# Alternating the two column halves of a tile's sums in the last matrix product of a decoder step

## The chip, the cores and the metric

The kernel runs on one core of a Trainium2 chip. The metric is the device time of one execution in microseconds (us); several executions are run and the median is quoted. One further execution was recorded by the hardware profiler, and all rows below are from it.

## The reference, cut to what matters

One decoder layer on 1024 prompt tokens and 32 sample tokens, `D_MODEL` 1024. It has a mixer part (gated linear attention beside a state-space model) and then PEER, a layer of 16384 single-neuron experts, of which each token uses 128. The change is in the second product of PEER:

```python
def block(args):
    xk, ik, gk = args
    act = jax.nn.gelu(jnp.einsum('tkd,td->tk', expert_u[ik], xk))
    return jnp.einsum('tk,tkd->td', gk * act, expert_v[ik])
...
x = x + peer_ffn(rmsnorm(x, norm2), peer_wq, peer_keys, peer_u, peer_v)
```

After it comes only the final RMSNorm of each token.

## The kernel before, in words

The first 2285 us hold the mixers, the expert scores, their top 16, and the first PEER product. They are not touched. The last part is `peer_down` (from L2347), about 1090 us.

**The product.** For six of the nine token tiles (ND = 6, 128 tokens each, the "dense" tiles) the kernel doesn't gather experts. It multiplies a weight matrix `w` (experts x tokens, mostly zeros) with the table `peer_v` (experts x 1024). The 16384 experts are 128 blocks of 128. Four blocks (GE = 4, counted by e) make a group, so there are 32 groups (NG, counted by g). In a group each dense tile s has 1024 sums for each of its tokens, which are two halves of 512 columns (W4), as a PSUM bank holds 512. So a group has 12 outputs (OUTS), numbered o = 2s + half. For each output and block there are three products (PARTS): every float32 operand is split into a high part h and a low part l in the fp32r type, and h*h, h*l and l*h are summed. That makes 4 x 3 = 12 products of 128x512 for each output, 144 in a group, 4608 in all. The stationary operand (the weight that PE loads) is the slice of `lo_wx` for the tile, the moving operand is half a row of `lo_vx`. The profile gives each product its own LDWEIGHTS record (engine PEld). Buffers come in two sets: even groups use lo_wx0 to 3 with up_ut2, up_ut0, up_ut1 and lo_vx3; odd groups use lo_wx4 to 7 with lo_vx4 to 7.

**PE's order** is written out in `peer_down`. Output after output, it waits until the bank is free (semaphore `o_added`; there are NPO = 6 banks `pd_po`), issues the 12 products and raises `o_done` with the last one. Ahead of each group it waits until VectorE (DVE) has made the low parts of all four blocks of that group: `v_lo` and `w_lo` must reach 4(g+1). Group 0 is a little different: its first six outputs run block by block.

**DVE's order** is also written out: for each group g and each output o (a "slot") one instruction that prepares group g+1, then the sum, then perhaps a gathered row:

```python
for g in range(NG):
    for o in range(OUTS):
        m = GE * (g + 1) + o // 3
        if g == 0:
            add(g, o)
        if m < NK:
            (lower.multiply, lower.low_v, lower.low_w)[o % 3](dve, m)
        if g >= 1:
            add(g, o)
        at = OUTS * g + o - FIRST_ROW
        for i in range(rows_by(at), rows_by(at + 1)):
            rows_v.add(dve, i, gate, acc_s)
```

`multiply` (L2132) forms `w` times the activations, `low_v` (L2147) the low part of a block of `peer_v`, `low_w` (L2152) the low part of `w`. `add` (L2471) waits for `o_done` of its output and adds the bank to `acc` in SBUF. `rows_v.add` (L1818) adds one gathered row of 1024 columns for the sparse tiles; 288 rows are spread evenly over 354 slots, from slot 0 of group 1 on. The last preparation for group g+1 is `low_w` in slot 11 of group g, right ahead of `add(g, 11)` and behind `add(g, 10)`.

**The others.** ScalarE (ACT) makes the high parts (L2137, L2141), SyncE (SP) loads `peer_v`, `w` and the activations, GpSimd (POOL) gathers the rows. In the last group nothing is left to prepare; PE first folds the sample tile with a small product (L2550), and DVE and ACT do the final norm of finished tiles between the sums, and of the last tile behind the last sum.

Of the kernel before, what the change touches and what calls it, by code (L numbers as in the profile page):

```python
# [11 lines left out]
F32R = mybir.dt.float32r  # L12
I32 = mybir.dt.int32
U32 = mybir.dt.uint32

P = 128
D = 1024
# [17 lines left out]
W4 = 512  # L35
# [1327 lines left out]
PARTS = ((0, 0), (0, 1), (1, 0))  # L1363
# [6 lines left out]
ND = 6  # L1370
# [467 lines left out]
def peer_topk(nc, s_sb, sel_t, u_d, up, lead, xs, idx, gate, raw):  # L1838


    with ExitStack() as ctx:
        def sb(name, shape, dt=F32):
            return ctx.enter_context(nc.sbuf_tensor("tk_" + name, shape, dt))
# [6 lines left out]
        top = sb("top", [P, PH, 2, TOPK])  # L1850
        ids = sb("ids", [P, PH, 2, TOPK], U32)
        idxf = sb("idxf", [P, PH, 2, TOPK])
        fin = sb("fin", [P, PH, TOPK])
        pos = sb("pos", [P, PH, TOPK], U32)
        pos2 = sb("pos2", [P, 2, PH, TOPK], U32)
        posf = sb("posf", [P, 2, PH, TOPK])
# [3 lines left out]
        sums = sb("sums", [P, PH])  # L1860
        idx_s = sb("idx_s", [P, NSEL], U32)
        gate_s = sb("gate_s", [P, NSEL])
# [219 lines left out]
GE = 4  # L2082
# [239 lines left out]
OUTS = 2 * ND  # L2322
# [16 lines left out]
def peer_down(nc, v_d, up, lead, lower, x2_tiles, acc, acc_s, idx, gate, raw, final_norm, y_tiles):  # L2339


    with ExitStack() as ctx:
# [3 lines left out]
        def sem(name):  # L2346
            return new_sem(nc, "pd_" + name)  # L2347

        lower.place(ctx, nc)
        vx, wx, mul, v_lo, w_lo = lower.vx, lower.wx, lower.mul, lower.v_lo, lower.w_lo  # L2350
        rows_v = Rows(ctx, nc, "dr", v_d, idx, 0, COLS, [lead.room[:, b] for b in range(3)], 2)
        NPO = 6
        po = [ctx.enter_context(nc.psum_tensor(f"pd_po{b}", [P, W4], F32)) for b in range(NPO)]
# [10 lines left out]
        o_done, o_added = sem("o_done"), sem("o_added")  # L2364
# [8 lines left out]
        @block.sync  # L2373
        def _(sp):
            def load(m):
                if m % 2 == 0 and m >= 4:
                    sp.wait_ge(w_lo, m - 2)
                    lower.load_wa(sp, m // 2)
                sp.wait_ge(v_lo, m - 1)
                lower.load_v(sp, m)  # L2380

            def load_acc(s):
                sp.dma_start(acc[:, s, :], x2_tiles[s]).then_inc(acc_in[s], 16)  # L2383

            load(2)
            load_acc(0)
            load(3)
            load_acc(1)
            up.keep(sp, NK - 1, 1)
            load_acc(2)  # L2390
            load(4)
            load_acc(3)
            load(5)
            load_acc(4)
            load_acc(5)
            up.all_kept(sp)
            load(6)
            load(7)
            for s in range(NSP):
                sp.dma_start(acc_s[:, s, :], x2_tiles[ND + s]).then_inc(accs_in, 16)  # L2400
            sp.wait_ge(accs_zero, 1)
            sp.dma_start(acc_s[0:TS, NSP, :], x2_tiles[NT - 1]).then_inc(accs_in, 16)
            for m in range(2 * GE, NK):
                load(m)
            sp.wait_ge(rows_v.used, COLS)
            sp.dma_start(gain, final_norm.rearrange("(o d) -> o d", o=1).broadcast_to([P, D])).then_inc(gain_loaded, 16)
            for i, s in enumerate(FINAL):
                sp.wait_ge(ready, i + 1)
                sp.dma_start(y_tiles[s], tile(s)).then_inc(written, 16)
            sp.wait_ge(written, 16 * NT)  # L2410
# [113 lines left out]

        @block.tensor
        def _(pe):
            def product(g, o, e):
                s, half = o // 2, o % 2
                for x, y in PARTS:
                    mm = nc.tensor.matmul(po[(OUTS * g + o) % NPO][:], wx[g % 2][e][y][:, s * P:(s + 1) * P],  # L2530
                                          vx[g % 2][e][x][:, half * W4:(half + 1) * W4],
                                          start=(e == 0 and (x, y) == PARTS[0]), stop=(e == GE - 1 and (x, y) == PARTS[-1]))
                return mm


            for e in range(GE):
                pe.wait_ge(v_lo, e + 1)
                pe.wait_ge(w_lo, e + 1)
                for o in range(NPO):
                    mm = product(0, o, e)  # L2540
                    if e == GE - 1:
                        mm.then_inc(o_done, 1)
            for g in range(NG):
                pe.wait_ge(v_lo, GE * (g + 1))
                pe.wait_ge(w_lo, GE * (g + 1))
                if g == NG - 1:
                    pe.wait_ge(shaped, PACK)
                    pe.wait_ge(rows_v.used, COLS)
                    for half in range(2):
                        nc.tensor.matmul(pf[half][0:TS, :], fold[:], acc_s[:, NSP, half * W4:(half + 1) * W4],  # L2550
                                         start=True, stop=True).then_inc(folded, 1)
                for o in range(NPO if g == 0 else 0, OUTS):
                    at = OUTS * g + o
                    if at >= NPO:
                        pe.wait_ge(o_added, at - NPO + 1)
                    for e in range(GE):
                        mm = product(g, o, e)
                    mm.then_inc(o_done, 1)


def mixers(nc, A, O, x_tiles, x2_tiles, ss2, lead):
# [24 lines left out]
def build(nc, A, O):  # L2586
# [10 lines left out]
    with nc.allow_non_contiguous_dma(reason="biases and S5 parameters, a few kilobytes"):  # L2597
        x2_order, y_order = [x2_tiles[t] for t in ORDER], [y_tiles[t] for t in ORDER]
        with ExitStack() as ctx:
# [4 lines left out]
            LIVE_SEMS.extend(lead.sems())  # L2604
            idx = ctx.enter_context(nc.sbuf_tensor("idx", [P, COLS], U32))
            gate = ctx.enter_context(nc.sbuf_tensor("gate", [P, COLS], F32))
# [48 lines left out]
```

## Time and profile before

| | us |
|---|---|
| three runs | 3372.06, 3375.76, 3374.07 |
| median | 3374.07 |
| profiled execution, its time | 3376.34 |
| its span | 3374.6 |
| PE busy in the span | 3285.9 (97%) |
| PEld busy | 2880.1 (85%) |
| DVE busy | 2551.5 (76%) |
| ACT, POOL busy | 901.1, 801.1 |
| granted TensorE clock, mean | 0.989 |

The busy time of PE counts each product from its start to its modelled end. Neighbouring products overlap, so a busy PE may still leave room, and the pace is read from the distance between two starts. The time outside the span is 1.74 us.

### The profile page before, as it was taken

The page shows a single profiled execution, that of the slowest core. Times are in us where ns is not written, and L with a number is a line of the kernel's source. Part 1 is how long each engine was busy: PE and PEld are TensorE (multiplying, and loading weights), DVE is VectorE, ACT ScalarE, POOL GpSimd, SP SyncE. Part 2 cuts the span into 40 slices and gives each one's busy share as a digit, 9 for nine tenths or more (in the row PEclk, how much of TensorE's full clock was granted, in tenths as well). Part 3 has the DMA queues.
Part 4 walks back from the last instruction along what each step waited for, and adds up shares of the span by engine and source line. Part 5 has one row for each costly group of instructions (what it writes and reads, how often), then busy time and mean ns, then how long its engine had stood idle before and what let it go on. Part 6 is the DMA issues. An engine that isn't in the chain of part 4 may idle for free. (4 is left out here: it accounts for less than half of the span.)

```text
span 3374.6 us, 46048 instructions
## 1 busy us (share of the span) xinstructions
PE 3285.9 (97%) x17796; PEld 2880.1 (85%) x17796; DVE 2551.5 (76%) x5349; ACT 901.1 (27%) x1310; POOL 801.1 (24%) x625
## 2 busy tenths in 40 slices
PE   8999989899999999999999999999999999999998
PEld 7867755499999999999999999997878888878787
DVE  6611253422499999989899888967999999999996
ACT  4210300211122222224444444432222222222222
POOL 0000000000001010113333333332444444444440
PEclk9999989899999999999999999999999999999999
DMA  3020021321144444448888888889899998988983
GB/s 98 14 39 27 13 91 59 119 57 38 55 136 136 147 144 145 137 150 303 289 316 309 287 326 285 329 310 339 309 307 312 311 311 310 311 315 309 312 307 132
DMA packets 332962, 695.58 MB, mean 206 GB/s; under 512 B 34332, under 2 KB 194936, under 8 KB 326584
## 3 DMA queue, kind: packets, MB, share of 16 engines
q1 hardware_dynamic: 248600, 386.28, 33.8%
q0 software_dynamic: 84144, 306.35, 26.4%
q8 instruction: 141, 2.31, 0.3%
q14 instruction: 77, 0.63, 0.1%
HBM read 580.10 MB, written 110.64 MB: 205 GB/s over the span
## 5 line engine op out<-in xcount | busy, mean ns | idle before, releaser
L1775 ACT ACTIVATE up_a<-up_pa 128x384 f32<-128x384 f32 x256 | 126.0, 492 | 838.9 <-PE up_pa L1760 829.2
L1799 POOL DMA_INDIRECT lead<-in_peer_v_dram,idx x174 | 259.7, 1492 | 361.8 <-DVE acc_s L1818 333.9
L2471 DVE TENSOR_TENSOR acc<-pd_po,acc 128x512 f32<-128x512 f32 x384 | 264.0, 688 | 101.6 <-PE pd_po L2530 97.4
L1799 POOL DMA_INDIRECT gr_row<-in_peer_u_dram,idx x192 | 229.0, 1193 | 374.4 <-DVE raw L1808 347.4
L1808 DVE CUSTOM_DVE_ANT_0 gr_row<-gr_row,xs 128x1024 f32<-128x1024 f32 x192 | 231.2, 1218 | 2.2 <-DMA gr_row<-in_peer_u_dram,idx 2.2
L1799 POOL DMA_INDIRECT dr_row<-in_peer_v_dram,idx x114 | 171.1, 1501 | 218.7 <-DVE acc_s L1818 215.3
L1818 DVE SCALAR_TENSOR_TENSOR acc_s<-lead,gate,acc_s 128x1024 f32<-128x1024 f32 x174 | 222.0, 1276 | 0.0
L2257 DVE TENSOR_SCALAR pg_hot_i<-pg_iota,sel_t 128x128 f32<-128x128 f32 x768 | 213.2, 353 | 0.0
L2292 PE MATMUL pg_pw<-pg_hot_i,pg_hot_j 128*128 128x128 f32 x1536 | 199.7, 275 | 1.5 <-DVE pg_hot_i L2257 1.5
L502 PE MATMUL fr_a<-pj_w,h_t 128*128 128x256 f32 (+1 forms) x864 | 200.0, 394 | 0.9 <-PEq L177 0.9
L502 PEld LDWEIGHTS fr_a<-pj_w,h_t 128*128 128x128 f32 (+1 forms) x864 | 170.9, 227 | 29.6 <-issue 8.2
L2292 PEld LDWEIGHTS pg_pw<-pg_hot_i,pg_hot_j 128*128 128x128 f32 x1536 | 192.5, 191 | 1.8 <-DVE pg_hot_i L2257 1.8
L2252 DVE TENSOR_TENSOR pg_hot_j<-pg_iota,sel_t 128x512 f32<-128x512 f32 x192 | 132.2, 688 | 79.2 <-PE pg_pw L2292 73.6
L1799 POOL DMA_INDIRECT lead<-in_peer_u_dram,idx x72 | 92.9, 1291 | 378.5 <-DVE raw L1808 302.8
L1750 PE MATMUL up_pt<-up_ident,lead 128*128 128x128 f32 x1024 | 134.9, 273 | 18.2 <-DVE up_ut1l L1780 4.5
L1818 DVE SCALAR_TENSOR_TENSOR acc_s<-dr_row,gate,acc_s 128x1024 f32<-128x1024 f32 x114 | 145.5, 1276 | 0.0
L1760 PE MATMUL up_pa<-h_dh,up_ut1h 128*128 128x384 f32 x688 | 140.8, 346 | 2.1 <-PEq L62 2.1
L1760 PE MATMUL up_pa<-h_dh,up_ut0h 128*128 128x384 f32 x688 | 140.8, 346 | 0.0
L1750 PEld LDWEIGHTS up_pt<-up_ident,lead 128*128 128x128 f32 x1024 | 117.3, 141 | 24.4 <-DMA lead<-in_peer_u_dram 5.4
L1760 PE MATMUL up_pa<-h_dh,up_ut2h 128*128 128x384 f32 x672 | 137.5, 346 | 0.0
L1760 PE MATMUL up_pa<-h_dh,up_ut1l 128*128 128x384 f32 x688 | 135.5, 339 | 0.0
L1760 PE MATMUL up_pa<-h_dh,up_ut0l 128*128 128x384 f32 x688 | 135.5, 339 | 0.0
(469 smaller groups left out, 7921.8 us busy)
## 6 DMA issues: line engine op xcount, KB each, us to landing
lead<-in_peer_u_dram SPq DMA_DIRECT2D x128, 512.0 KB, 4.9
room<-in_peer_v_dram SPq DMA_DIRECT2D x128, 512.0 KB, 4.7
act_d<-up_a SPq DMA_DIRECT2D x256, 192.0 KB, 3.0
room<-w_d SPq DMA_DIRECT2D x64, 768.0 KB, 6.9
room<-act_d SPq DMA_DIRECT2D x64, 768.0 KB, 9.7
w_d<-room SPq DMA_DIRECT2D x24, 1024.0 KB, 10.6
w_d<-pg_wb SPq DMA_DIRECT2D x24, 1024.0 KB, 9.4
pj_w<-in_w_in_dram SPq DMA_DIRECT2D x8, 1024.0 KB, 6.2
```

The source lines that it names most:

```text
L502: mm = nc.tensor.matmul(out, h_t[:, k, tok], w[piece % 2][:, k, :], start=(k == 0), stop=(k == KD - 1))
L1750: mm = self.nc.tensor.transpose(self.pt[half][:, k * P:(k + 1) * P], self.u_sb[n % 2][:, c:c + P], self.ident[:])
L1760: mm = self.nc.tensor.matmul(self.pa[c][:, 0:WB], self.ut[n % self.NB][x][:, k, :], self.h[y][:, k, c * WB:(c + 1) * WB], start=(i == 0), ...
L1775: self.nc.scalar.activation(self.a_sb[c][:], self.pa[c][:, 0:WB], ACT.Gelu_apprx_tanh).then_inc(self.a_act, 1)
L1799: pool.indirect_dma_start(self.buf[i % self.n], None, self.table, bass.IndirectOffsetOnAxis(ap=self.idx[:, col:col + 1], axis=0)).then_inc ...
L1808: self.nc.vector.tensor_tensor_reduce(row, row, xs[:, col // NSEL, :], 1.0, 0.0, ALU.mult, ALU.add, raw[:, col:col + 1]).then_inc(self.use ...
L1818: self.nc.vector.scalar_tensor_tensor(out=out, in0=self.buf[i % self.n], scalar=w[:, col:col + 1], in1=out, op0=ALU.mult, op1=ALU.add).the ...
L2252: nc.vector.tensor_tensor(hot_j[:, hb], iota[:].unsqueeze(1).broadcast_to([P, BT, P]), sel_t[:, 1, g * BT:(g + 1) * BT].unsqueeze(2).broad ...
L2257: ins = nc.vector.tensor_scalar(hot_i[:, hb, j, :], iota[:], sel_t[:, 0, tok], sel_t[:, 2, tok], ALU.is_equal, ALU.mult)
L2292: mm = nc.tensor.matmul(pw[g % 2][:, j, :], hot_j[:, g % NHB, j, :], hot_i[:, g % NHB, j, :], start=True, stop=True)
L2471: nc.vector.tensor_tensor(out, po[(OUTS * g + o) % NPO][:], out, ALU.add).then_inc(o_added, 1)
```

## The change

Only the instruction order of PE in `peer_down` changes, and where it waits and signals. The two halves of a tile now alternate: product (x, y) of block e for half 0, the same for half 1, then the next (x, y). Both halves have the same weight, so PE loads each weight twice in a row, with its own LDWEIGHTS each time. A pair of banks is open at once, so PE waits for both to be free (`at - NPO + 2`, with `at` even), and `o_done` is raised by the last product of half 0 and by the last product of half 1, which are the last two of the pair's 24. (An unused type name is added at the top, which moves the line numbers by one.)

```diff
-            def product(g, o, e):
-                s, half = o // 2, o % 2
+            def products(g, s, e):
                 for x, y in PARTS:
-                    mm = nc.tensor.matmul(po[(OUTS * g + o) % NPO][:], wx[g % 2][e][y][:, s * P:(s + 1) * P],
-                                          vx[g % 2][e][x][:, half * W4:(half + 1) * W4],
-                                          start=(e == 0 and (x, y) == PARTS[0]), stop=(e == GE - 1 and (x, y) == PARTS[-1]))
-                return mm
+                    done = []
+                    for half in range(2):
+                        done.append(nc.tensor.matmul(po[(OUTS * g + 2 * s + half) % NPO][:], wx[g % 2][e][y][:, s * P:(s + 1) * P],
+                                                     vx[g % 2][e][x][:, half * W4:(half + 1) * W4],
+                                                     start=(e == 0 and (x, y) == PARTS[0]),
+                                                     stop=(e == GE - 1 and (x, y) == PARTS[-1])))
+                return done
...
-                for o in range(NPO if g == 0 else 0, OUTS):
-                    at = OUTS * g + o
+                for s in range(NPO // 2 if g == 0 else 0, ND):
+                    at = OUTS * g + 2 * s
                     if at >= NPO:
-                        pe.wait_ge(o_added, at - NPO + 1)
+                        pe.wait_ge(o_added, at - NPO + 2)
                     for e in range(GE):
-                        mm = product(g, o, e)
-                    mm.then_inc(o_done, 1)
+                        done = products(g, s, e)
+                    done[0].then_inc(o_done, 1)
+                    done[1].then_inc(o_done, 1)
```

The block-by-block start of group 0 changes in the same way. The order of DVE, ACT, POOL and SP is the same as before.

PE at the end of group 0 and the start of group 1, before. The semaphores `o_added`, `v_lo` and `w_lo` are printed under the names that their numbers had in an earlier stage: fr_swept, n1_x_loaded7 and n1_x_loaded4.

```order
L2530 MATMUL pd_po<-lo_vx3l,lo_wx3h 128x512
L2530 MATMUL pd_po<-up_ut2h,lo_wx0h 128x512 [waits fr_swept]
L2530 MATMUL pd_po<-up_ut2h,lo_wx0l 128x512
L2530 MATMUL pd_po<-up_ut2l,lo_wx0h 128x512
L2530 MATMUL pd_po<-up_ut0h,lo_wx1h 128x512
L2530 MATMUL pd_po<-up_ut0h,lo_wx1l 128x512
L2530 MATMUL pd_po<-up_ut0l,lo_wx1h 128x512
L2530 MATMUL pd_po<-up_ut1h,lo_wx2h 128x512
L2530 MATMUL pd_po<-up_ut1h,lo_wx2l 128x512
L2530 MATMUL pd_po<-up_ut1l,lo_wx2h 128x512
L2530 MATMUL pd_po<-lo_vx3h,lo_wx3h 128x512
L2530 MATMUL pd_po<-lo_vx3h,lo_wx3l 128x512
L2530 MATMUL pd_po<-lo_vx3l,lo_wx3h 128x512
L2530 MATMUL pd_po<-lo_vx4h,lo_wx4h 128x512 [waits fr_swept,n1_x_loaded7,n1_x_loaded4]
```

The second row starts output 11; its twelve products are all for one bank, and the 12th is the last of the group. The same place of the changed kernel:

```order
L2533 MATMUL pd_po<-up_ut2h,lo_wx0l 128x512 x2
L2533 MATMUL pd_po<-up_ut2l,lo_wx0h 128x512 x2
L2533 MATMUL pd_po<-up_ut0h,lo_wx1h 128x512 x2
L2533 MATMUL pd_po<-up_ut0h,lo_wx1l 128x512 x2
L2533 MATMUL pd_po<-up_ut0l,lo_wx1h 128x512 x2
L2533 MATMUL pd_po<-up_ut1h,lo_wx2h 128x512 x2
L2533 MATMUL pd_po<-up_ut1h,lo_wx2l 128x512 x2
L2533 MATMUL pd_po<-up_ut1l,lo_wx2h 128x512 x2
L2533 MATMUL pd_po<-lo_vx3h,lo_wx3h 128x512 x2
L2533 MATMUL pd_po<-lo_vx3h,lo_wx3l 128x512 x2
L2533 MATMUL pd_po<-lo_vx3l,lo_wx3h 128x512 x2
L2533 MATMUL pd_po<-lo_vx4h,lo_wx4h 128x512 [waits fr_swept,n1_x_loaded7,n1_x_loaded4]
```

Each row marked x2 is one product for output 10 and one for output 11. Output 10, which was complete twelve products ahead of the end of the group, is now complete one product ahead of it. The wait for the next group stands where it stood.

DVE around the change of a group (here the slots 10 and 11 of one group and the slot 0 of the next), the same in both kernels; the line numbers are those of before:

```order
L2147 TENSOR_TENSOR lo_vx7l<-room,lo_vx7h 128x1024
L2471 TENSOR_TENSOR acc<-pd_po,acc 128x512
L1818 SCALAR_TENSOR_TENSOR acc_s<-lead,gate,acc_s 128x1024
L2152 TENSOR_TENSOR lo_wx7l<-room,lo_wx7h 128x768
L2471 TENSOR_TENSOR acc<-pd_po,acc 128x512
L1818 SCALAR_TENSOR_TENSOR acc_s<-dr_row,gate,acc_s 128x1024
L2132 TENSOR_TENSOR room<-room 128x12x64
```

The first L2471 is `add(g, 10)`, the second is `add(g, 11)`, and between them stand a gathered row and the `low_w` that PE needs before it may start group g+1. Nothing moved here; what moved is when the first L2471 may start.

## Rows read from the trace of the kernel before

**Rows 1.** Page, part 4: the chain that ended last, by engine
```profile
PE 31%; DMA 0%; DVE 0%; issue 0%; SPq 0%; ACT 0%; DVEq 0%
```

**Rows 2.** The chain in order of time: start us, length us, what
```profile
2321.03 1.56 issue
2322.59 35.65 PE pd_po L2530 x144
2358.24 0.85 issue
2359.09 33.76 PE pd_po L2530 x144
2392.85 0.10 issue
2392.94 32.92 PE pd_po L2530 x144
2425.86 0.38 issue
...
3299.80 31.33 PE pd_po L2530 x135
3331.14 1.83 PE up_pa L2550 x4
3332.97 32.92 PE pd_po L2530 x144
```

**Rows 3.** Stretches (busy us of PE, PEld, DVE, ACT, POOL; clock; DMA share; GB/s)
```profile
2359.00:3331.00 972.00, 965.03 (x4176) 781.82 (x4176) 889.90 (x976) 215.17 (x235) 412.18 (x275) 1.00 0.88 304
2322.00:2329.00 7.00, 6.41 (x16) 5.08 (x17) 0.49 (x1) 0.00 (x0) 0.00 (x0) 0.54 1.03 405
```

**Rows 4.** Waits of PE, then of DVE, 2359 to 3331 us (total us, times, longest)
```profile
PE pd_po L2530 <- issue: 7.5, 23, 0.9
```
```profile
DVE acc L2471 <- PE pd_po L2530: 79.9, 87, 1.7
```

**Rows 5.** Timeline, end of group 12: start us, length us, what [idle before]
```profile
2727.72 0.39 PE L2530 MATMUL pd_po<-lo_vx3h,lo_wx3l 128*128 128x512 f32 x1
...
2727.94 0.39 PE L2530 MATMUL pd_po<-lo_vx3l,lo_wx3h 128*128 128x512 f32 x1
...
2728.59 0.47 PE L2530 MATMUL pd_po<-lo_vx4h,lo_wx4h 128*128 128x512 f32 x1 [0.26 <-issue]
```

**Rows 6.** Timeline of DVE over the same group's end
```profile
2724.60 1.22 DVE L2147 TENSOR_TENSOR lo_vx7l<-room,lo_vx7h 128x1024 fp32r<-128x1024 f32 x1
2725.74 0.68 DVE L2471 TENSOR_TENSOR acc<-pd_po,acc 128x512 f32<-128x512 f32 x1
2726.34 1.28 DVE L1818 SCALAR_TENSOR_TENSOR acc_s<-lead,gate,acc_s 128x1024 f32<-128x1024 f32 x1
2727.53 0.95 DVE L2152 TENSOR_TENSOR lo_wx7l<-room,lo_wx7h 128x768 fp32r<-128x768 f32 x1
2728.40 0.69 DVE L2471 TENSOR_TENSOR acc<-pd_po,acc 128x512 f32<-128x512 f32 x1
```

**Rows 7.** Timeline of DVE at the end of group 14, no row in slot 10
```profile
2792.97 0.68 DVE L2471 TENSOR_TENSOR acc<-pd_po,acc 128x512 f32<-128x512 f32 x1
2793.57 0.95 DVE L2152 TENSOR_TENSOR lo_wx7l<-room,lo_wx7h 128x768 fp32r<-128x768 f32 x1
2795.59 0.69 DVE L2471 TENSOR_TENSOR acc<-pd_po,acc 128x512 f32<-128x512 f32 x1 [1.08 <-PE pd_po L2530]
```

**Rows 8.** Timeline, the last product and the last sum
```profile
3365.49 0.39 PE L2530 MATMUL pd_po<-lo_vx7l,lo_wx7h 128*128 128x512 f32 x1
3365.91 0.69 DVE L2471 TENSOR_TENSOR acc<-pd_po,acc 128x512 f32<-128x512 f32 x1 [2.03 <-PE pd_po L2530]
```

**Rows 9.** Timeline of PE: behind its two longest idle times, and where banks change
```profile
2285.27 0.47 PE L2530 MATMUL pd_po<-up_ut2h,lo_wx0h 128*128 128x512 f32 x1 [2.50 <-PEq L2172]
2285.58 0.39 PE L2530 MATMUL pd_po<-up_ut2h,lo_wx0l 128*128 128x512 f32 x1
...
2286.49 0.39 PE L2530 MATMUL pd_po<-up_ut2l,lo_wx0h 128*128 128x512 f32 x1
2286.71 0.39 PE L2530 MATMUL pd_po<-up_ut2h,lo_wx0h 128*128 128x512 f32 x1
...
2318.45 0.39 PE L2530 MATMUL pd_po<-lo_vx3l,lo_wx3h 128*128 128x512 f32 x1
2322.59 0.77 PE L2530 MATMUL pd_po<-lo_vx4h,lo_wx4h 128*128 128x512 f32 x1 [3.75 <-issue]
...
2327.85 0.63 PE L2530 MATMUL pd_po<-lo_vx4h,lo_wx4h 128*128 128x512 f32 x1
2328.27 0.45 PE L2530 MATMUL pd_po<-lo_vx4h,lo_wx4l 128*128 128x512 f32 x1
```

**Rows 10.** Timeline of DVE, the sum of output 10 of group 0
```profile
2319.20 0.69 DVE L2471 TENSOR_TENSOR acc<-pd_po,acc 128x512 f32<-128x512 f32 x1
```

More of the change, by code:

```diff
@@ L14 @@
 U32 = mybir.dt.uint32
+U16 = mybir.dt.uint16
 P = 128
@@ L2538, in _ @@
                 pe.wait_ge(w_lo, e + 1)
-                for o in range(NPO):
-                    mm = product(0, o, e)
+                for s in range(NPO // 2):
+                    done = products(0, s, e)
                     if e == GE - 1:
-                        mm.then_inc(o_done, 1)
+                        done[0].then_inc(o_done, 1)
+                        done[1].then_inc(o_done, 1)
             for g in range(NG):
@@ L2551, in _ @@
                                          start=True, stop=True).then_inc(folded, 1)
-                for o in range(NPO if g == 0 else 0, OUTS):
-                    at = OUTS * g + o
+                for s in range(NPO // 2 if g == 0 else 0, ND):
+                    at = OUTS * g + 2 * s
                     if at >= NPO:
-                        pe.wait_ge(o_added, at - NPO + 1)
+                        pe.wait_ge(o_added, at - NPO + 2)
                     for e in range(GE):
-                        mm = product(g, o, e)
-                    mm.then_inc(o_done, 1)
+                        done = products(g, s, e)
+                    done[0].then_inc(o_done, 1)
+                    done[1].then_inc(o_done, 1)
 def mixers(nc, A, O, x_tiles, x2_tiles, ss2, lead):
```

## The prediction

> **What bounds the kernel now.** I read the chain that ended last first: DVE and DMA have 0% of it, PE of this product alone 31% [rows 1]. In order of time the chain is one group of 144 products after the other, with an "issue" gap of 0 to 0.85 us between groups [rows 2]. So in the last 1090 us the time is the pace of the products times their number, plus what is lost at each change of group. The pace: a group's run lasts 33.76 us in the even buffer set and 32.92 us in the odd one [rows 2]. Less the 0.39 us of the last product and divided by 143, starts are 233.4 and 227.5 ns apart, mean 230.5. The granted clock is 1.00 (2.4 GHz) over the whole stretch [rows 3].
>
> DVE is the second engine: 889.9 us busy in 972 [rows 3], and it idles 79.9 us for the products [rows 4], all of it waiting in `add`. It has 2.7 us to spare in a group, so the order in which it is served matters. PE idles 7.5 us in 23 of the 29 changes of group [rows 4]. What it waits for is seen in one of them. The last product of group 12 starts at 2727.94, the first of group 13 at 2728.59 [rows 5], and the one thing that ends in between is `lo_wx7l`, the last preparation, at 2727.53 + 0.95 = 2728.48 [rows 6]. PE starts 0.11 us behind it. That preparation stands behind `add(g, 10)` on DVE: sum at 2725.74, row at 2726.34, `low_w` at 2727.53. Before the change this chain of 2.85 us starts when output 10 is done and runs beside the 12 products of output 11 (12 x 0.23 = 2.8 us). It is covered almost exactly.
>
> **The change, part by part.**
>
> *Products and loads.* Number, shape and operands stay; 4608 products with 4608 loads. Nothing is skipped because a weight comes twice. The trace has no place where these products have the same weight twice. I take the pace as unchanged. Bounds: it can't be under the stream itself, 512 columns at 2.4 GHz = 213.3 ns, 17.2 ns less than the mean. Upwards the nearest row is a change of bank after every third product in group 0: 2286.49 to 2286.71, 0.22 us [rows 9], no more than between products of one bank. So 0, with -17.2 ns as the far end.
>
> *The signal of output 10.* It is now raised by the second-last product of the group. A sum starts 0.42 us behind the start of its last product (3365.49 to 3365.91 [rows 8]), so `add(g, 10)` starts 0.42 - 0.23 = 0.19 us behind the start of the group's last product. From there the chain is serial: sum to row 0.60, row to `low_w` 1.19, `low_w` 0.95, to the product 0.11 [rows 5, 6]. The first product of the next group starts 3.04 us behind the last one, against a normal 0.23: 2.81 us lost. Nothing covers it, as PE has no other work that may go ahead. Where slot 10 has no row, DVE goes from the sum to `low_w` in 0.60 [rows 7], and 1.62 us are lost. By the formula for 288 rows over 354 slots, slot 10 is empty in the groups 1, 10, 14, 18, 22 and 30.
>
> *Sum for the changes behind group 2 to 29.* 24 with a row, 24 x 2.81 = 67.4; 4 without, 6.5; together 73.9. Today the same 28 lose the 7.5 us of idle time, plus 0.39 - 0.23 = 0.16 us for each of 23, as the profile counts idle time from the modelled end: 11.2. Difference **+62.7**.
>
> *The others.* Behind group 1: 1.62 instead of 0.85 + 0.16, +0.6. Behind group 30, where today there is no gap: +1.6. Behind group 0: the last product there starts at 2318.45, and PE then waits 3.75 us [rows 9], since DVE is late by itself: the sum of output 10 starts at 2319.20, in DVE's own turn [rows 10]. In pairs output 10 is done at 2318.6, still ahead of that turn. 0.
>
> *Waits for banks in pairs.* PE needs both sums of the pair three pairs back, that is two pairs (11 us) after that pair was done. DVE gets to the second sum in 0.60 + 1.19 + 1.14 + 0.60 = 3.5 us [rows 6]. 0.
>
> *DVE between pairs.* With two rows in a pair its work is 2 x 0.60 + 2 x 1.19 + 1.14 + 0.87 = 5.6 us [rows 6], against 24 products of 5.6 us (even) or 5.46 us (odd). It is late by 0.15 us now and then at the end of an odd group, up to 0.3; some 7 such places, +1.4.
>
> *DMA, ACT.* They follow the pace of DVE; ACT's first high part of a group waits for the end of the group before last, as today. 0.
>
> *The end.* Both last sums now stand behind the last product: 0.19 + 0.60 instead of 0.42, +0.4.
>
> Total 62.7 + 0.6 + 1.6 + 1.4 + 0.4 = **+66.7 us**. The profiled span would be 3374.6 + 66.7 = 3441.3. The median of the runs shown is 0.5 us under that span (and 2.3 under the profiled time), so I forecast 3374.07 + 66.7, about **3441 us**, 2% slower. A measurement of this kernel can tell about 0.2% (7 us) from no change.
>
> **The rivals.**
>
> *A. The serial gap, pace as now:* 3441. For it: every term is a measured duration, the order of DVE doesn't change, and the present gaps are just what the same chain gives when 2.8 us of it are covered. Bounds: if the 24 rows in the chain cost nothing, 24 x 1.19 = 29 less (3412); if DVE is late by a further 0.5 us at each change, 15 more (3456). The durations of all five links are read, so I put A's own range at 3428 to 3456, half of the way down.
>
> *B. The repeated weight brings the products closer, so far that the gap is paid for.* It ends on the other side. Mechanism: part of the 17.2 ns above the stream is the change of weight in the array, and falls away for the second of each two. If for every product, 4464 x 17.2 ns = 77 us, and the time would be 3364; for every second one 38 us, and 3403. It needs over 14.9 ns of the 17.2 for each product to be not slower. Against it: the load record is there for each product, 188 ns long, busy 781.8 us of 972 [rows 3], and it already fits beside the product ahead; also a change of the moving operand or the bank shows no cost. The Trainium skill (TensorE: Matmul & The Clock Gate, "Back-to-back issue gap") has a spacing of about 216 ns for a lone stream of 512 columns, and says that loads and products together set the spacing in a real kernel; by that figure, an estimate, the whole gain to be had is 4464 x 14.7 ns = 66 us, and no run here shows it.
>
> *C. The clock falls in the gaps.* The row behind the idle time of 3.75 us shows 14 products of 0.427 us, granted clock 0.54 with the rest of the stretch, before the pace of 0.23 comes back [rows 3, 9]. Behind 2.50 us of idle time the pace is 0.23 from the second product on [rows 9]. The new idle time is 3.04 - 0.39 = 2.65 us by the profile's count, just above the one that was harmless. If the clock fell in all 28 gaps, 28 x 14 x 0.20 = 78 us more, 3519; in a third of them 3467. The Trainium skill (TensorE: Matmul & The Clock Gate, "HAM oscillation") warns of just this, a pause between bursts that halves the clock each time; the row of 3.75 us agrees, that of 2.50 us says that this one may be short enough.
>
> *D. The change has no effect* since DVE or DMA catches up elsewhere: 3374. Against: DVE can't start the sum of a product that isn't done, and DMA isn't in the chain.
>
> **How the numbers follow.** A 0.80. C 0.09, most of it in part of the gaps. B 0.09: 0.06 for a small gain of 2 to 5 ns (3441 - 9 to 22), 0.03 for one of 13 to 17. D 0.02. The range of 3418 to 3470 takes in A with its bounds, the small form of B and C in a third of the gaps, and leaves out some 0.13. Faster by over 0.2% needs B nearly in full, 0.02. Within 0.2%: the rest of large B, and D, 0.03. Slower 0.95.
>
> **What would show it.** In the chain every change of group should have a gap: "issue", or DVE by name, with about 2.65 us (1.2 to 1.3 in four), and DVE in the order sum, row, `low_w` right behind the last product. PE's waits should sum to 70 to 75 us in 28 to 30 times, and DVE's for `pd_po` grow to some 145 us, in steps of up to 2.6 us at the first pair of a group. Runs of 144 products should keep 33.76 and 32.92 us. B would be seen in shorter runs, or in unequal steps inside a pair. C would be seen as a clock under 1.00, and 0.43 us steps behind each gap. I am wrong if the gaps are there but under 2 us, which would mean that the row isn't in the chain, or if the runs of 144 change by over 0.5 us.

## The result and the profile after

The changed kernel takes 3479.85 us in the median of four runs (3473.22 to 3481.28), the kernel before 3374.68; the ratio is 1.031, 95% interval 1.0295 to 1.0324. That is 105 us slower, where I forecast 67, and 10 us above my range. The granted clock is 0.977 in the profiled execution, 0.989 before. The direction and the gaps came as forecast, and the clock did what rival C said, at a lower price for each gap.

The page of the changed kernel gives the busy time of each engine. Against the table of before PE is busy 38.6 us longer for the same 17796 products:

```profile
PE 3324.5 (96%) x17796; PEld 2909.4 (84%) x17796; DVE 2546.4 (73%) x5349; ACT 899.3 (26%) x1310; POOL 801.9 (23%) x625
```

The chain that ended last, by engine, answers to [rows 1], and the same chain in order of time (start us, length us, what) to [rows 2]:

```profile
PE 30%; issue 3%; DVE 2%; DVEq 0%; ACT 0%
```
```profile
2359.41 1.56 issue
2360.96 33.58 PE pd_po L2533 x144
2394.54 2.67 issue
2397.21 32.92 PE pd_po L2533 x144
2430.13 2.67 issue
2432.80 35.13 PE pd_po L2533 x144
2467.93 2.70 issue
```

Every change of group now has its gap. It is 2.67 us by the profile's count, up to 2.97 where DVE is late, and 1.5 us where slot 10 has no row. The second thing to see is in the lengths of the runs. Those at 2360.96 (even set) and 2397.21 (odd set) are as before within 0.2 us, 33.58 and 32.92. The run at 2432.80 (even set) takes 35.13 us for the same 144 products, which is over the 0.5 us that I had named as a sign of being wrong.

The waits of PE and then of DVE over the groups 2 to 30 (2361 to 3434 us; total us, times, longest), which answer to [rows 4]:

```profile
PE pd_po L2533 <- issue: 73.5, 29, 3.0
```
```profile
DVE acc L2472 <- PE pd_po L2533: 186.2, 84, 5.9
```

PE's 73.5 us lie in the 70 to 75 that I named. DVE's 186 us are well over my 145. In run 1 below, where the gaps are the same and the clock stays up, they are 151.8, so most of the excess is DVE waiting for slow products.

The timeline at a change of group with a row in slot 10 (behind group 11), which answers to [rows 5, 6]: start us, length us, what.

```profile
2727.64 0.39 PE L2533 MATMUL pd_po<-lo_vx7l,lo_wx7h 128*128 128x512 f32 x1
2727.84 0.69 DVE L2472 TENSOR_TENSOR acc<-pd_po,acc 128x512 f32<-128x512 f32 x1 [0.80 <-PE pd_po L2533]
...
2728.45 1.28 DVE L1819 SCALAR_TENSOR_TENSOR acc_s<-lead,gate,acc_s 128x1024 f32<-128x1024 f32 x1
2729.64 0.95 DVE L2153 TENSOR_TENSOR lo_wx3l<-room,lo_wx3h 128x768 fp32r<-128x768 f32 x1
...
2730.70 0.65 PE L2533 MATMUL pd_po<-up_ut2h,lo_wx0h 128*128 128x512 f32 x1 [2.67 <-issue]
```

The sum starts 0.20 us behind the last product, then come the row, `low_w` and PE: 3.06 us from the start of the group's last product to the start of the next group's first, forecast 3.04. I call this figure the distance from here on; without any gap it is 0.23. The profile's idle time is 0.39 us shorter.

Where the rest went is seen behind such a gap. The timeline of PE (two products in a row marked x2):

```profile
2768.54 1.19 PE L2533 MATMUL pd_po<-lo_vx4h,lo_wx4h 128*128 128x512 f32 x2 [2.70 <-issue]
2769.53 1.06 PE L2533 MATMUL pd_po<-lo_vx4h,lo_wx4l 128*128 128x512 f32 x2
2770.38 1.06 PE L2533 MATMUL pd_po<-lo_vx4l,lo_wx4h 128*128 128x512 f32 x2
2771.24 0.88 PE L2533 MATMUL pd_po<-lo_vx5h,lo_wx5h 128*128 128x512 f32 x2
2771.96 0.62 PE L2533 MATMUL pd_po<-lo_vx5h,lo_wx5l 128*128 128x512 f32 x2
```

Up to about 2771.7 two products take 0.85 us instead of 0.46, a product 0.427 us (512 columns at 1.2 GHz). From the fifth pair on the old pace is back. Two stretches of one group each (busy us of PE, PEld, DVE, ACT, POOL; clock; DMA share; GB/s), the first without, the second with slow products:

```profile
2397.00:2430.00 33.00, 32.79 (x144) 26.95 (x144) 28.40 (x33) 6.24 (x7) 14.68 (x10) 1.00 0.84 287
2508.00:2543.00 35.00, 34.90 (x144) 28.10 (x144) 26.96 (x30) 6.23 (x7) 12.89 (x9) 0.95 0.85 282
```

Product by product over the groups 2 to 30: 24 changes of group have a distance of 3.05 us or more. Behind 23 of them 6 to 8 products (14 once) stand over 0.36 us apart, nearly all 0.427, the pace of 1.2 GHz. That costs some 1.55 us each time, 2.8 us for the 14. The slow stretch needn't start with the group: behind group 21 six steps are at full pace first. Behind the five distances of 1.9 to 2.2 us there is no slow product.

### The profile page after: what moved, and what is told of

Read it like the earlier page. It is cut to its first block and busy times, and to the rows that moved or that the text cites. A ratio compares the mean times of both kernels' runs of the same rounds, so it can differ in the third digit from the quotient of the medians.

```text
span 3479.5 us, 46048 instructions
## 1 busy us (share of the span) xinstructions
PE 3324.5 (96%) x17796; PEld 2909.4 (84%) x17796; DVE 2546.4 (73%) x5349; ACT 899.3 (26%) x1310; POOL 801.9 (23%) x625
## 3 DMA queue, kind: packets, MB, share of 16 engines
q1 hardware_dynamic: 248600, 386.28, 33.1%
```

## The experiments

The theory: the loss has two parts and both come from PE standing still at the change of group. (1) The serial chain on DVE, 67 us. (2) The clock that falls in or just behind the gap, 38 us. The rival: it is alternating itself (one weight twice, two open banks) that costs the pace or the clock, in part or in full. None of the ten kernels below leaves out any of the computation; the edits change order, signals and, in two, add products that nobody reads.

**1. The gap filled with idle work.** Six small products into a bank that is not read, ahead of PE's wait:

```diff
             for g in range(NG):
+                if g >= 2:
+                    for _ in range(6):
+                        nc.tensor.matmul(pf[0][:, 0:P], gate[:, 0:P], gate[:, 0:P], start=True, stop=True)
                 pe.wait_ge(v_lo, GE * (g + 1))
```

> The changed kernel with six small float32 products (128x128, of the gate values, into a bank that nobody reads) at the end of each group, ahead of PE's wait for the next one. They add about 1.6 us of work inside the gap of 2.8 us and change nothing else. If the clock falls because PE stands idle in the gap: the gaps stay, the slow products vanish, about 3441 to 3446. If the slow products come from something else that goes with the group's start (the alternation, DVE's traffic): 3480 as in the changed kernel, or more.

3440.74 us (3439.64 to 3443.23), ratio to before 1.0198 (1.0181 to 1.0215), clock 0.989. The timeline of PE at one change of group:

```profile
2428.38 0.61 PE L2533 MATMUL pd_po<-lo_vx7l,lo_wx7h 128*128 128x512 f32 x2
2428.84 1.50 PE L2551 MATMUL up_pa<-gate 128*128 128x128 f32 x12
2431.66 0.70 PE L2533 MATMUL pd_po<-up_ut2h,lo_wx0h 128*128 128x512 f32 x2 [1.33 <-issue]
2432.20 0.62 PE L2533 MATMUL pd_po<-up_ut2h,lo_wx0l 128*128 128x512 f32 x2
```

The trace lists each small product as two records, so the six of them are the x12. The next group starts no earlier, the distance is 3.05 us as in the changed kernel, and the product behind it is at full pace. From group 2 on no group has slow products. More work on PE, and 39 us less: this is the price of the clock, by itself. In the two profiled executions the groups 2 to 30 differ by 36.9 us inside the groups and by under 0.1 us in the distances. What is left, 3440.7, is the 3441 that I had worked out for the gaps alone.

**2. One signal moved in the kernel before.** No alternation anywhere; only output 10 is signalled with output 11:

```diff
-                    mm.then_inc(o_done, 1)
+                    if o == OUTS - 1:
+                        mm.then_inc(o_done, 2)
+                    elif o != OUTS - 2:
+                        mm.then_inc(o_done, 1)
```

> The kernel before, with one semaphore moved: output 10 of each group is signalled only with output 11. All products stay in the order of before. Gap theory: the gap is 0.23 us longer than in the changed kernel, 3.27 us with a row in slot 10 and 2.1 without, so 3374 + 67 + 6 = 3447 by the gaps alone, and the clock falls behind most of them as in the changed kernel, 37 to 45 us more: about 3487. Rival (it is the alternation that lowers the clock): 3447, clock 0.989.

3486.70 us (3484.83 to 3492.76), ratio 1.0341 (1.0322 to 1.0361), clock 0.978. The distances are 3.28 us, and 2.08 without a row. A single late signal gives the whole loss; the order of the products is not needed for it. With the six small products of run 1 added to this kernel:

> late_signal (products as before, output 10 signalled with output 11) with the six small products of the run filler in each gap. If the slow clock is only PE's idleness: gaps of 3.28 us stay, no slow products behind them, 3374 + 73 = 3447 to 3450, clock 0.989. If in late_signal something else lowers it: 3487.

3446.86 us (3440.65 to 3448.49), ratio 1.0207 (1.0186 to 1.0229), clock 0.989. The distances stay at 3.28, no group from 2 on has slow products, where the trace of late_signal has them behind 19 of 24 (6 to 8 products, 13 or 14 in four cases). Again 40 us for the clock between the medians; in the two traces the groups differ by 33.9 us.

**3. A shorter gap.** The changed kernel; DVE takes the row of slot 10 behind the sum of output 11:

```diff
                     at = OUTS * g + o - FIRST_ROW
-                    for i in range(rows_by(at), rows_by(at + 1)):
+                    here = range(rows_by(at), rows_by(at + 1))
+                    if o == OUTS - 2:
+                        here = range(0)
+                    if o == OUTS - 1:
+                        here = range(rows_by(at - 1), rows_by(at + 1))
+                    for i in here:
```

> The changed kernel, but DVE takes the gathered row of slot 10 only behind the sum of output 11, so that the sum of output 10 is followed at once by the last preparation. Gap theory: every gap is 1.9 us (1.54 by the profile's count), the kind behind which the changed kernel kept its clock six times of six. So 28 x 1.62 = 45 less the 11 of before, plus 4 at the ends: 3374 + 38 = 3412, clock 0.989. If the clock falls for another reason than the length of the gap: some 3447, clock 0.977.

3413.47 us (3409.30 to 3414.42), ratio 1.0114 (1.0096 to 1.0132), clock 0.988. Distances of 1.86 to 2.16 us behind all groups from 1 to 29, and no slow product behind any of them. The 66 us against the changed kernel are 28 for the rows taken out of the chain (24 x 1.19) and the rest for the clock.

Then half of the row in slot 10 and half behind the sum of output 11:

> The changed kernel with the row of slot 10 in two halves of 512 columns, the second half behind the sum of output 11. The gap becomes 0.19 + 0.60 + 0.60 + 0.95 + 0.11 = 2.45 us, between the 1.9 that never lost the clock and the 3.05 that nearly always did. By the gaps alone 3374 + 53 = 3427. If the clock holds there: 3425 to 3430, clock 0.989. If it falls behind all: 3462.

3455.41 us (3454.54 to 3456.44), ratio 1.0239 (1.0219 to 1.0259), clock 0.982. The distance is 2.52 us (2.55 to 2.82 where DVE is late), and behind 17 of 24 such gaps the products are slow. 17 x 1.55 = 26 us on top of 3427 gives 3453. So the clock can fall in a gap that the profile counts as under 2.2 us idle; the same length sometimes loses it and sometimes not. The waits of PE in this kernel, from 2361 to 3330 us:

```profile
PE pd_po L2549 <- issue: 54.5, 26, 2.4
```

**4. Which of the pairs matters.** First all tiles but the last alternate:

```diff
                 for s in range(NPO // 2 if g == 0 else 0, ND):
...
+                    if s == ND - 1:
+                        for half in range(2):
+                            for e in range(GE):
...
+                            mm.then_inc(o_done, 1)
+                        continue
                     for e in range(GE):
                         done = products(g, s, e)
```

> The changed kernel, but the two halves of the last tile of each group (outputs 10 and 11) run one after the other as before; the other five tiles alternate. Gap theory (the loss is the serial gap behind each group, and the clock that falls in it): outputs 10 and 11 are signalled as before, the gaps shrink to 0 to 0.9 us, the clock is back at 0.989, and the time is 3375, within 5 of before. Rival (alternating halves with a repeated weight and two open banks is itself slower, or lowers the clock): five sixths of the 39 us that the gap doesn't explain remain, about 3405, with slow products somewhere in the groups.

3434.86 us (3434.32 to 3441.84), ratio 1.0188 (1.0168 to 1.0208), clock 0.988. This is a miss for both: 60 us over my 3375. The timeline of DVE in one group shows why (slots 8 to 11):

```profile
2450.70 0.69 DVE L2472 TENSOR_TENSOR acc<-pd_po,acc 128x512 f32<-128x512 f32 x1 [1.08 <-PE pd_po L2533]
2451.31 1.28 DVE L1819 SCALAR_TENSOR_TENSOR acc_s<-lead,gate,acc_s 128x1024 f32<-128x1024 f32 x1
2452.50 0.95 DVE L2133 TENSOR_TENSOR room<-room 128x768 f32<-128x768 f32 x1
2453.37 0.68 DVE L2472 TENSOR_TENSOR acc<-pd_po,acc 128x512 f32<-128x512 f32 x1
2453.97 1.27 DVE L1819 SCALAR_TENSOR_TENSOR acc_s<-lead,gate,acc_s 128x1024 f32<-128x1024 f32 x1
2455.16 1.22 DVE L2148 TENSOR_TENSOR lo_vx7l<-room,lo_vx7h 128x1024 fp32r<-128x1024 f32 x1
2456.30 0.68 DVE L2472 TENSOR_TENSOR acc<-pd_po,acc 128x512 f32<-128x512 f32 x1
2456.90 1.27 DVE L1819 SCALAR_TENSOR_TENSOR acc_s<-lead,gate,acc_s 128x1024 f32<-128x1024 f32 x1
2458.09 0.95 DVE L2153 TENSOR_TENSOR lo_wx7l<-room,lo_wx7h 128x768 fp32r<-128x768 f32 x1
```

Output 10 was done by 2453.7 here, as its last product started at 2453.28. DVE didn't wait for it; it came to it at 2456.30, because the pair of outputs 8 and 9 had been given to it only at 2450.70 and is followed by 5.6 us of work. The gap is the same 3.07 us, by another way. Where a slot without a row stands ahead, DVE catches up by 1.2 us, so the distances are 1.9, 2.16, 3.07, 3.2 and 3.35. Only 12 are of 3.07 or more, and 8 of these lose the clock.

Then the two opposite cases, only the last tile and only the first tile of each group alternating:

> The changed kernel, but only the last tile of each group (outputs 10 and 11) alternates; the other five run as before. Gap theory, with DVE waiting for the pair when it comes: DVE is not late at output 10, so each gap is the full 3.05 us (1.9 without a row in slot 10): by the gaps alone 3374 + 66 = 3440, and the clock falls behind most of them, so 3470 to 3482. If the loss came from alternating as such, a sixth of it is left: about 3392.

3476.62 us (3470.37 to 3482.27), ratio 1.0305 (1.0279 to 1.0332), clock 0.979. One tile of six gives the whole loss; 22 of 24 gaps of 3.05 us have slow products behind them, and so has the one of 2.52 behind group 1.

> The changed kernel, but only the first tile of each group alternates. After last_tile_plain the theory is that a pair delays DVE by the 2.8 us for which it can't start the first sum, and that DVE, with hardly any time to spare, carries that on to the end of the group unless slots without a row let it catch up. From the first pair it has ten slots to do so: gaps of 0.5 to 1.2 us instead of 0 to 0.9, 3381, clock 0.989. If the position in the group didn't matter: about 3392 as in a sixth of the loss, or 3435 if one pair costs as much as five.

3380.47 us (3378.39 to 3386.12), ratio 1.0018 (1.0008 to 1.0028), clock 0.990. From group 2 on the distances are 0.5, 0.65 and 1.16 us (0.23 once), without slow products; the one behind group 1 is 3.79, with eight slow products, where DVE starts its last preparation only 2.7 us behind PE's last product (2353.80 against 2351.06); why it is late there is open. The place in the group decides: from the first pair DVE has ten slots, one or two of them without a row, to come back. The same sixth of the products costs 102 us at the end and 6 at the beginning.

**5. The cause removed on DVE.** From group 1 on DVE takes both preparations of a pair of slots ahead of the pair's first sum. Once with PE's order of the changed kernel, once with that of before:

```diff
-                    if m < NK:
+                    if g == 0 and m < NK:
                         (lower.multiply, lower.low_v, lower.low_w)[o % 3](dve, m)
+                    if g >= 1 and o % 2 == 0:
+                        for n in (o, o + 1):
+                            if GE * (g + 1) + n // 3 < NK:
+                                (lower.multiply, lower.low_v, lower.low_w)[n % 3](dve, GE * (g + 1) + n // 3)
```

> The changed kernel with DVE's order matched to it: from group 1 on both preparations of a pair of slots stand ahead of the first sum of the pair, so the last preparation for the next group no longer stands behind the sum of output 10. PE's order is that of the changed kernel. Gap theory: no gap behind groups 1 to 30 but DVE's own lateness (under 0.3 us), clock 0.989; 3374 less the 11 us that the gaps cost before, plus 0.4 at the end: about 3364. If the alternation has a price of its own, it shows here against the run of the same DVE order with PE's order of before: the difference of the two.

> The kernel before with the same order of DVE as in prep_ahead_pairs, PE's order untouched. The present gaps of 0 to 0.65 us go: 3374 - 11 = 3363, clock 0.989. Compared with prep_ahead_pairs it gives what the alternation of the halves costs or brings by itself: 0 within 3 us by my pace term; up to 77 us in favour of pairs if a repeated weight were cheaper.

With the alternating halves 3365.70 us (3362.92 to 3369.74), ratio to before 0.9976 (0.9966 to 0.9987). With PE's order of before 3360.71 us (3353.18 to 3364.70), ratio 0.9961 (0.9947 to 0.9974). Both have the clock at 0.989, and both beat the kernel before; the second is the best of all. The timeline of DVE in the first, at a change of group:

```profile
2420.83 1.23 DVE L2148 TENSOR_TENSOR lo_vx3l<-room,lo_vx3h 128x1024 fp32r<-128x1024 f32 x1
2421.96 0.96 DVE L2153 TENSOR_TENSOR lo_wx3l<-room,lo_wx3h 128x768 fp32r<-128x768 f32 x1
2423.84 0.69 DVE L2472 TENSOR_TENSOR acc<-pd_po,acc 128x512 f32<-128x512 f32 x1 [0.92 <-PE pd_po L2537]
```

The last preparation is done, and DVE still waits 0.92 us for output 10. PE's waits from 2361 to 3330 us are 1.1 us in 7 times:

```profile
PE pd_po L2537 <- issue: 1.1, 7, 0.2
```

With single outputs PE has no wait there at all. Inside a group the two orders have the same pace: from the first to the last start 33.1 to 33.2 us (even) and 32.4 to 32.5 (odd) with pairs, 33.2 and 32.4 with single outputs. So a weight that comes twice in a row, and banks that alternate with every product, bring nothing and cost nothing here, to within 0.1 us in a group. The 5 us between the medians are not the pace. In the profiled executions group 2 starts 4.1 us later with pairs (2357.77 against 2353.68), of which 2.1 lie ahead of the stage, and which I have not taken apart further. From there to group 31 it is 964.9 against 963.2 us: with pairs DVE is late by a fraction of a microsecond at some 16 changes of group (distances of 0.42 to 0.55), 3.9 us together, and 0.5 us slower inside the groups, while the single order has 13 slow products in group 2, 2.7 us, behind a distance of 3.51.

## Why the prediction was wrong

*Bound and mechanism:* right. The time is the pace of the products plus what is lost at each change of group, and the signal of output 10 made a covered chain serial. Runs 1 and 2 show it from both sides.

*The sum of the gaps:* right. Distance forecast 3.04 and 1.85 us, measured 3.05 and 1.93. The total of 66.7 us was measured when the clock was held up: 3440.74 - 3374.19 = 66.6 us in run 1. That it agrees to 0.1 us is in part luck. In that trace the distances behind the groups 2 to 29 grew by 65.4 us, forecast 62.7 + 1.4, the second for DVE's lateness. Of the 11.2 us that I took as today's loss, the gap behind group 1 was one, and I counted it again by itself; from start to start it is 10.7. Against this the pairs are 1.1 us faster inside the groups 2 to 30. The start, which I put at 0, hides two changes that cancel: group 0 takes 1.2 us more and group 1 takes 1.2 us less, as it has 7 slow products instead of 13.

*Pace unchanged, repeated weight worth nothing:* right; rival B is out by run 5.

*The clock:* this is the step that failed. The sum had no term for it, and rival C had only 0.09. I put the row with 2.50 us of idle time ahead of the row with 3.75 [rows 9] and took the forecast gap of 2.65, "just above the one that was harmless", as harmless too. One row in which the clock stayed shows only that it can stay. In the changed kernel 23 of 24 such gaps lost it, and in the half-row run 17 of 24 of a shorter kind. The missing term is 39 us (3479.85 - 3440.74). It is half of what C named (78): the number of times was nearly right, 23 instead of 28, but behind these gaps mostly 6 to 8 products are slow, not the 14 that followed the idle time of 3.75 us. With this term the sum is 3374 + 67 + 39 = 3480, but only after the fact, as the 39 are measured.

The row of 2.50 us was itself a lucky one. That idle time, ahead of the first product of the stage, is in all twelve traces, and the code ahead of it is the same in all. In eleven it is 2.33 to 2.55 us, and in six of these the clock falls behind it; in the changed kernel it is 3.10, and the clock falls too. Two that lost it, at the place of the first two lines of [rows 9], from late_signal_filler, where the sixth product is the first to be slow, and from prep_ahead_single, where it is slow at once (its PE order is that of before):

```profile
2283.54 0.47 PE L2530 MATMUL pd_po<-up_ut2h,lo_wx0h 128*128 128x512 f32 x1 [2.42 <-PEq L2172]
...
2284.78 0.54 PE L2530 MATMUL pd_po<-up_ut2l,lo_wx0h 128*128 128x512 f32 x1
2285.11 0.63 PE L2530 MATMUL pd_po<-up_ut2h,lo_wx0h 128*128 128x512 f32 x1
2285.54 0.63 PE L2530 MATMUL pd_po<-up_ut2h,lo_wx0l 128*128 128x512 f32 x1
```
```profile
2280.77 0.57 PE L2534 MATMUL pd_po<-up_ut2h,lo_wx0h 128*128 128x512 f32 x1 [2.45 <-PEq L2172]
2281.14 0.63 PE L2534 MATMUL pd_po<-up_ut2h,lo_wx0l 128*128 128x512 f32 x1
2281.57 0.63 PE L2534 MATMUL pd_po<-up_ut2l,lo_wx0h 128*128 128x512 f32 x1
```

The warning of the Trainium skill that I cited (TensorE: Matmul & The Clock Gate, "HAM oscillation": a pause between bursts halves the clock each time) is what happened here in 23 of 24 gaps. The section's own case has pauses of 3 to 5 us. Here pauses of 2.1 to 3.0 us of idle time were enough in most cases, and the measurement decides: none of the 29 distances of 1.86 to 2.16 us in run 3 lost the clock.

*DVE between pairs:* its term of 1.4 us was right (1.6 measured over the 24 gaps with a row), but I had not seen that DVE's lateness carries a pair's delay over to the next outputs. Without that the run last_tile_plain was foretold 60 us too low. In the changed kernel itself it makes no difference, as the last pair is delayed anyway.

## What to carry to other kernels

When two outputs are merged so that both are signalled late, follow the in-order consumer from that signal to the next thing that the producer waits for; the cost is that whole chain, once for every turn of the loop, and the place of the late signal in the turn counts for more than how many there are. Put preparations for the next turn ahead of the consumer's waits on the current one: here that was worth 0.4% against the old kernel with PE's old order, and 0.2% with the pairs. And price a new regular gap on TensorE twice, for its length and for the slow products behind it; unless rows show many gaps of that length without them, the second price belongs in the sum.

## What the runs showed of the hardware

- Gaps of 2.5 to 3.4 us from product to product can cost the clock, with 6 to 8 products (13 or 14 in seven cases) of 0.427 us behind them and some 1.55 us each time. The slow stretch starts with the first product or up to six products later. Among gaps of one length it fell behind 23 of 24, 22 of 24 and 19 of 24 (3.05 to 3.4 us) and 17 of 24 (2.5 to 2.8 us), and behind none of 1.9 to 2.2 us. What tells two gaps of equal length apart is open; ahead of the stage idle times of 2.33 to 2.55 us behind the same instructions lost the clock in six executions of eleven.
- Work that nobody needs, 1.5 us of small products in each gap, made the changed kernel 39 us faster. It left 1.33 us of idle time in a gap of 3.05.
- Consecutive products with the same weight and alternating banks have the pace of products with different weights in one bank (run 5, within 0.1 us in a group of 144), 227 and 232 ns for 512 columns in the two buffer sets. Why the two sets differ by 5 ns was not tried.
